# VectorE's order inside a pair of output tiles: the weight sums of the next pair ahead of the first result operation

## What is computed

```python
xn = rms_norm(x, p['norm'])
proj = xn @ p['w_in']
(a_u, a_v, a_z, b_cq, b_ckv, b_kpe, b_z,
 c_h, c_b, c_c, c_z, gates) = jnp.split(proj, IN_SPLITS, axis=-1)
...
g = jax.nn.sigmoid(gates.astype(jnp.float32)).astype(x.dtype)
h = (g[..., 0, :] * (ya @ p['w_pa']) + g[..., 1, :] * (yb @ p['w_pb'])
     + g[..., 2, :] * (yc @ p['w_pc']))
return x + h @ p['w_out'], ckv_new, kpe_new, conv_new, a_vn
```

## Time and profile before

| | us |
|---|---|
| median of 3 runs | 6791.76 |
| lowest, highest | 6788.22, 6793.39 |
| the profiled execution's own time | 6785.36 |
| its span on the slowest core (7) | 6783.6 |
| spans of the 8 cores | 6754.7 to 6783.6 |
| TensorE busy in the span | 6417.8 |
| VectorE busy in the span | 3642.1 |

### The profile page before, as it was taken

The page is one execution under the profiler, slowest core; times in us unless marked ns, Lnnn a source line. Parts: engine busy times, 40 slices in busy tenths (PEclk is TensorE's granted clock), DMA queues, the critical chain, the costliest instruction groups (busy, mean ns, idle before and its releaser), DMA issues.

```text
span 6783.6 us, 117138 instructions; the slowest of 8 cores (6754.7 to 6783.6 us)
## 1 busy us (share of the span) xinstructions
PE 6417.8 (95%) x40156; PEld 3774.5 (56%) x40156; DVE 3642.1 (54%) x6406; ACT 2468.8 (36%) x5376; POOL 670.5 (10%) x1008
## 2 busy tenths in 40 slices
PE   3998999999799899999899999999999999999998
PEld 1654788777455488777644445444434444544443
DVE  4665566556566556555644344555465444455545
ACT  2665331112376522111137673211124767321110
POOL 0002300002000310000200001000020000100000
PEclk9999999999899999999999999999999999999999
DMA  5333454446433254444742223444474222354446
GB/s 114 74 76 63 77 86 79 82 80 145 113 69 77 53 95 85 76 81 82 201 107 42 49 44 61 83 78 78 81 162 108 43 46 43 66 81 78 81 78 155
DMA packets 175648, 571.41 MB, mean 84 GB/s; under 512 B 20056, under 2 KB 34392, under 8 KB 175072
## 3 DMA queue, kind: packets, MB, share of 16 engines
q0 software_dynamic: 120784, 426.31, 37.3%
q1 hardware_dynamic: 54288, 137.61, 6.1%
HBM read 929.57 MB, written 60.53 MB: 146 GB/s over the span
## 4 chain that ended last, share of the span: by engine, by line
PE 82%; DVE 7%; issue 5%; DMA 4%; ACT 1%; SPq 1%; POOL 0%; DVEq 0%; ACTq 0%; POOLq 0%
PE ps L485 82%; DVE W L508 2%; DVE ct L508 1%; DMA xr<-x 1%; DVE R L511 1%; SPq L255 1%; DMA o_ckv<-F 1%; DMA y<-xr 1%; DMA cfm<-cfm_d 0%; DMA xr<-xm 0%; ACT F L504 0%; DVE accx L508 0%; DVE ssS L1546 0%; DMA R2f<-x 0%; DMA b<-bias_d 0%
## 5 line engine op out<-in xcount | busy, mean ns | idle before, releaser
L485 PE MATMUL ps<-R,W 128*128 128x512 bf16 (+3 forms) x19296 | 3305.8, 327 | 22.2 <-DVE R L511 7.4
L485 PEld LDWEIGHTS ps<-R,W 128*128 128x128 bf16 x19296 | 1888.1, 98 | 1305.0 <-issue 78.7
L508 DVE TENSOR_TENSOR ct<-ps,ct 128x260 f32<-128x260 f32 (+1 forms) x1500 | 740.9, 511 | 922.1 <-PE ps L485 905.6
L255 POOL DMA_DIRECT2D W<-wst x796 | 425.0, 534 | 5907.4 <-PE ps L485 4865.6
L504 ACT ACTIVATE ct<-ps 128x260 f32<-128x260 f32 (+1 forms) x600 | 269.8, 456 | 1406.6 <-PE ps L485 1347.1
L485 PE MATMUL ps<-xs,W 128*128 128x260 bf16 (+1 forms) x4224 | 644.2, 309 | 59.5 <-DVE ct L508 59.4
L485 PEld LDWEIGHTS ps<-xs,W 128*128 128x128 bf16 x4224 | 399.8, 97 | 303.9 <-issue 122.8
L508 DVE TENSOR_TENSOR W<-W,W 128x1024 bf16<-128x1024 bf16 (+1 forms) x600 | 503.5, 866 | 20.8
L504 ACT ACTIVATE P<-ps 128x512 bf16<-128x512 f32 x768 | 426.3, 599 | 207.6 <-PE ps L485 202.5
L504 ACT ACTIVATE sg<-ct 128x520 bf16<-128x520 f32 (+1 forms) x384 | 242.5, 633 | 695.4 <-DVE ct L508 695.3
L485 PE MATMUL ps<-qpe,kp 128*128 128x512 bf16 (+2 forms) x1280 | 432.8, 349 | 0.0
(11 more groups left out here) (170 smaller groups left out, 6180.5 us busy)
## 6 DMA issues: line engine op xcount, KB each, us to landing
W<-wst POOLq DMA_DIRECT2D x796, 512.0 KB, 5.4
xr<-x SPq DMA_DIRECT2D x16, 520.0 KB, 13.4
xr<-xm SPq DMA_DIRECT2D x16, 520.0 KB, 8.0
y<-xr SPq DMA_DIRECT2D x16, 520.0 KB, 10.4
Vsc<-vcur SPq DMA_DIRECT2D x16, 512.0 KB, 4.1
Ksc<-kcur SPq DMA_DIRECT2D x32, 256.0 KB, 4.6
vpast<-Vsc SPq DMA_DIRECT2D x16, 512.0 KB, 3.9
kpast<-Ksc SPq DMA_DIRECT2D x32, 256.0 KB, 2.6
```

The costliest lines, as they stand in the source:

```text
L255: self.E[Q].dma_start(out=out, in_=in_, **kw).then_inc(self.sem[name], 16)
L485: S.op('pe', lambda e: e.matmul(out, lhsT=lhsT, rhs=rhs, start=start, stop=stop, skip_group_check=skip), [lhsT, rhs], [out], stop if inc i ...
L508: S.op(eng, lambda e: e.tensor_tensor(out=out, in0=a, in1=b, op=op), [a, b], [out], hold=0.1 + size(a) / (960 if eng == 'dve' else 300), l ...
```

## The change

`prep` no longer puts its four operations into `fq`, it returns them. `quad` puts H, H and D of the next pair into `fq` at its start, and a new `drain()` issues all that is in `fq` ahead of z and pz. S follows pz. The `fill` at the end of the pair is gone, so the last two closing operations of a pair are issued by the `drain()` of the next one (or of the stage).

```diff
-                fq.extend([half(0), half(1), diff, both])
+                return [half(0), half(1), diff, both]
...
+                ahead = prep(*nxt_) if nxt_ is not None else []
+                fq.extend(ahead[0:3])
                 a = banks()
                 prod(a, lambda k: y[:, 0, k, :], lambda k, s, w: x[:, 8 + k, H + s:H + s + w], True)
                 t1 = copy(a)
...
                 t2 = copy(c)
+                drain()
                 z = banks()
                 prod(z, lambda k: sa[:, k, :], lambda k, s, w: xs[0][:, k, s:s + w], True)
                 part(t1, z, t1, ALU.subtract)
-                if nxt_ is not None:
-                    prep(*nxt_)
-                fill(3)
+                fq.extend(ahead[3:])
+                fill(1)
                 q = banks()
                 prod(q, lambda k: x0[:, 0, k, :], lambda k, s, w: xs[3][:, k, s:s + w], True)
                 t = CT.get()
                 part(t, q, t2, ALU.add)
                 use(1, 0, t)
-                fill(1)
...
                 use(1, 1, t2)
-                fill(2)
...
-            prep(*seq[0])
+            fq.extend(prep(*seq[0]))
```

## The result

| | before | after |
|---|---|---|
| median of 4 runs each, us | 6789.99 | 6726.84 |
| lowest, highest | 6779.66, 6793.39 | 6725.5, 6730.95 |
| ratio after / before, 95% | | 0.9911 [0.9893, 0.9928] |

The change is 63 us faster, 0.9%. The direction was predicted, the size was not: the forecast was 6759 us with a range from 6746 to 6774, a gain of 32 us, so the gain was twice the forecast.

A forecast was written before the change was run, and what follows sets the result against it. TensorE, 95% busy, was taken as the bound, waiting 0.62 us for pq in tile 1's pairs. Gain -54.0, first `cz` pairs +12.0, first `wo` pairs +9.6 gave -32.4 us: 6759 us, range 6746 to 6774.

The forecast's parts named there:

- Pairs with the pattern of 0.62 us: Tile 1's z and g stages, passes 2 and 3: 84 pairs each lose TensorE's 0.62 us wait for pq, 52.1 us gained.
- there the wait just does not arise: Tile 0's pairs: q2 may enter pq's first bank early, so TensorE does not wait for pq and nothing is gained.
- The stages of tile 0 as long as before but for their first pair: Sign named for the profile after: tile 0's stages keep their length, except in their first pair.
- The first `cz` pairs: Start of each pass's z stage: sums ahead delay pz, costing 3.0 us per pair, 12.0 us in four passes.
- The fall of the clock: First `cz` pairs: about 4.0 us of TensorE idle lowers the granted clock, costing 1.7 us each, taken as due.
- The wo stages and what lies behind them: Wo stages: first pairs cost 9.6 us over three passes; three later pairs of pass 3 gain 1.9 us.
- The first `wo` pair: Start of the wo stage: z2 waits 7 to 8 us; cost 3.2 us in three passes, hidden in pass 1.
- 0.9 us more: Wo stages of passes 0 and 2: three sums beside POOL take 3.48 us in place of 2.61.
- (1): Rival: no clock fall at first `cz` pairs and pass 2's wo gains come; -41 us, 6751 us, chance 0.16.
- (2): Rival: in ordinary pairs the wait moves to z2; 6791.8 us less 0 to 10, chance 0.09 together with (4).
- (4): Rival: pq still waits, now behind S, so the path is unchanged; part of (2), chance 0.09 together.
- (3): Rival: sums stretch to 5.9 us in their new place in every pair; +303 us, 7095 us, chance 0.03.

The follow-up runs named there:

- The old order in tile 1 alone: The change, but tile 1's passes keep before's order (H, H and D behind pz, S behind pq); 0.9985 [0.9969, 1.0001] of before.
- in tile 0 alone: The change, but tile 0's passes keep before's order (H, H and D behind pz, S behind pq); 0.991 [0.9886, 0.9934] of before.
- the old order in the first `cz` pair alone: The change, but each pass's first `cz` pair has H, H and D behind pz, S behind pq; 0.9898 [0.9872, 0.9923] of before.
- the second execution: The changed kernel itself run once more, unaltered, on the chip of the later kernels, for its profile; 6716.5 us, a single time without a ratio.

## Why the prediction was half of it

**The step that failed first** is the gain: "Pairs with the pattern of 0.62 us ... 84 x 0.62 = 52.1". The count and the mechanism were right (no wait is left in those pairs; the sums fit into the gap with 0.70 us), the term was not: a pair lost 0.78 us, so it is 84 x 0.78 = 65.5, 13.4 more. The forecast pair period of 12.25 us came out as 12.09. The prediction's own numbers already held this: a pair of tile 1 is 56 matmuls, at its 0.216 us each 12.09 us, and the pairs were 12.87 apart.

**The second** is "in tile 0 ... there the wait just does not arise". It did, at 0.163 us in each of 84 ordinary pairs, 13.7 us. Two banks of 260 columns let q2 enter early, but not quite early enough. Both errors have one root: the idle column and the busy share were read as if TensorE's groups ended where their last matmul ends. "The stages of tile 0 as long as before but for their first pair" was the named check, and it failed.

These two are 27.1 us, beside 30.8 between the forecast gain and the measured one. The old order in tile 1 alone and in tile 0 alone show them apart, and the old order in the first `cz` pair alone shows their sum: 79.6 us where 52.1 was forecast.

**The first `cz` pairs:** the wait was right (3.96 us), q2's wait was won back, and the size was about right: 13.4 us as the mean of the eight cores, 12.1 in the second execution, against 12.0. The fall of the clock was taken as due in every pair, and came in 31 of 32; the one without it, core 2 in pass 2, cost 1.1 us, where the forecast had 1.3 for this case. Its price, taken as 1.7 us, was 1.3 to 1.7 in most pairs and 2.4 to 2.9 in the others. The 16.0 of core 7 is the top of the eight.

**The wo stages and what lies behind them:** forecast +9.6 - 1.9 = 7.7, by pass 3.2, 0, 3.2 and 1.3. From the first `wo` product of a pass to the next z stage (in pass 3 to the end) the means of the eight cores measured +6.6, -1.2, +6.6 and +0.5 us, +12.5 together, and +10.8 in the second execution. The first `wo` pair did as told, 7.74 us idle, and pass 1 hid it. Within the six pairs of passes 0 and 2 the change costs 9 us each: about 3 in the first pair, as forecast, and about 6 in the other five, beside POOL, where nothing was forecast; 2.4 of the 9 are hidden behind the pairs. The term that was too low is the part on POOL: it was taken at "0.9 us more" for three sums, and takes 2.5. Core 7 alone shows +2.6 us, but by the length of before: there core 7 took 2779 us in these four parts and the other seven 2761 to 2770.

**The sum,** means of the eight cores, 6767.2 to 6714.2 us:

| | forecast | measured |
|---|---|---|
| 84 ordinary pairs of tile 1 | -52.1 | -65.5 |
| 84 ordinary pairs of tile 0 | 0 | -13.7 |
| the one g pair more of each pass | 0 | -1.9 |
| first `cz` pairs, with the pair behind | +12.0 | +13.4 |
| wo stages and what lies behind | +7.7 | +12.5 |
| up to the first `cz` pair of pass 0, where nothing is changed | 0 | +2.3 |
| together | -32.4 | -52.9 |

The parts are cut from the same span, so that they add up proves nothing; the size of the pairs' gain is shown by the kernels above. The 63 us between the medians are 10 more than this mean. The time is that of the slowest core, and in the profiled execution of before it lay 16 us above the mean of the eight, after 12; the rest is how single executions of before differ, 6779.66 to 6793.39. The second execution of the change, on the chip of the later kernels, has 58 us less than this before as a mean. So as a mean of the cores the change is worth 53 to 58 us, and the rest of the 63 is which core was the slowest and which executions were timed.

**The rivals.** (1), no fall of the clock at the first `cz` pairs, came at one pair of 32 with the whole change; with H, H alone ahead it came at 3 of 16. (2), the wait moving to z2, and (4), S as the new obstacle, did not come in the z and g stages; in the wo stages of passes 0 and 2, beside POOL, z2 does wait 1.3 to 2.3 us in a pair, which is (2) in the one place where the sums stretch. (3) named the stretch and needed it in every pair; no single sum of the z and g stages was over 1.3 us.

## What to carry over

Read a wait of TensorE from start to start of its groups against the same group elsewhere (here 3.71 beside 3.55 and 4.24 beside 3.45 us); the idle column leaves out the overlap of pipelined matmuls, and hides a wait shorter than it entirely. Work that has slack goes ahead of the operation that is waited for where the engine idles anyway, and stays behind it at a stage's start, where the engine is late: one order for both cost 12 to 14 us here. Before a part of some 10 us is read from one core, read it on all eight: the first `cz` pairs cost 10.8 to 16.0 us in one execution. Before sums of two SBUF inputs are moved on VectorE, look what POOL does at the new place.

## What was new of the hardware

POOL's additions hold up VectorE's operations with two SBUF inputs: 2.61 us of sums took 5.09 beside 2.54 us of POOL, a single one up to 3161 ns, while operations with one input in PSUM stayed at 0.68 to 0.69. Of the 78.5 us by which VectorE's busy time rose, the weight sums, and so this, are 19.

The clock does not follow the length of an idle time alone. Behind 3.96 us it fell on core 5, and on core 2 of the same execution, at the same pair, it stayed at 1.00. Behind 2.63 us at one pair it fell on core 2 and stayed up on core 3. What else decides was not tried.
